# A two-way state-space stage: backward states turned in place, entering products read from the states, block-local kernels laid out twice in memory

## The chip, the cores and the metric

One Trainium2 chip, one of its cores. The metric is the device time of one execution in microseconds; the time before is the median of three runs. The kernel is one launch that holds a whole two-layer encoder trunk.

## The reference, cut to what matters

The trunk is an attention layer and then a two-way diagonal state-space layer over 1024 prompt and 256 sample tokens of width 1024. Only the second layer's core is concerned. For each of 64 groups of 16 channels a scan runs forward and another backward over the tokens:

```
bu_re = einsum('btgc,gpc->btgp', uc, bb_re)      # and bu_im
_, _, hr, hi = associative_scan(_complex_affine_combine, (ar_full, ai_full, bu_re, bu_im), axis=1)
y = einsum('btgp,gcp->btgc', hr, c_re) - einsum('btgp,gcp->btgc', hi, c_im)
...
y = (y_fwd + y_bwd) + d * u
gl = gelu(y);  y = gl * sigmoid(gl @ w_glu + b_glu) * silu(z)
```

## The kernel before, in words

`ssm_stage` (line 1291) takes the tokens in columns of L = 8, so 160 columns: 128 of the prompt, 32 of the sample. One group's 8 x 16 inputs of a column fill 128 partitions. What a column adds to its own 8 outputs is a product with a 128 x 128 "near" kernel; what comes from other columns passes through 64 complex states of each direction.

**First half.** TensorE projects the tokens in 16 tiles of weights (eight of u, then eight of z), each in three chunks of tokens and three products of split float32 numbers. ScalarE casts each tile's weights (`w_split`, line 1477); the low parts are subtracted by GpSimd for tiles 0 to 9 and by VectorE for tiles 10 to 15. Each u block of eight groups is stored, read back with 8 x 16 inputs on the partitions, and multiplied into the states that leave each column (`leaving`, line 1612); ScalarE copies the forward half into partitions 0 to 63 of `states`, VectorE the backward half, columns reversed, into partitions 64 to 127. From tile 9 on TensorE also makes the near kernels (`kernels`, line 1627): 16 turns q of four groups, one after each chunk. ScalarE copies a turn out, GpSimd adds the skip term, and SyncE (SP) stores it in `kernel_scratch` and then loads what turn q + 2 needs.

**The scan.** VectorE walks 127 columns (lines 1570 to 1598), both directions at once, prompt and sample together for the first 31. A step is four dependent operations on a column, which lies as 2 x 64 floats, 512 bytes, so a state's next column is 512 bytes further. The walk pauses at steps 0, 12, 31, 43, 59 and 75 for the low weights of tiles 10 to 15; at each pause VectorE waits for ScalarE's cast.

**Second half.** Work goes in 24 joints, three to a block of eight groups (3, 3 and 2 groups). A joint is a near product per group (line 1674: moving u, stationary near kernel, whose weights lie 16 bytes apart) and two entering products per group (line 1691: stationary `e`, moving the entering states). Each joint has a PSUM bank, so the near products of the first eight joints run ahead of the scan's end. For the entering products ScalarE gathers the forward states of a joint from `states` into `en` (`entering`, line 1512) and VectorE the backward states, turned round (lines 1599 to 1608), two joints ahead. Then come gelu and the stores.

SP's order (lines 1421 to 1463) sets when the loads of the second half start: three groups of near kernels, each of eight DMAs to 16 partitions (line 1409), u again block by block (line 1404), the `e` blocks (line 1416), and the stores of y.

Of the kernel before, what the change touches and what calls it, by code (L numbers as in the profile page):

```python
# [54 lines left out]
L = 8  # L55
# [1220 lines left out]
TURN = 4  # L1276
QG = 4
# [13 lines left out]
def ssm_stage(nc, w_d, h_scratch, skip_d, f_scratch, e_scratch, bb_scratch, c0_scratch, decay_scratch,  # L1291
              u_scratch, z_scratch, kernel_scratch, y_scratch):
# [10 lines left out]
    with ExitStack() as ctx:  # L1303
# [8 lines left out]
        with ExitStack() as first:  # L1312
# [26 lines left out]
        en = out_u[:].rearrange("p a t -> p (a t)")[:, 0:2 * PART * 2 * NC]\  # L1339
            .rearrange("p (b g r n) -> p b g r n", b=2, g=PART, r=2)  # L1340
# [9 lines left out]
        k_done, k_out, k_skip, k_stored = (m.sem(n) for n in ("k_done", "k_out", "k_skip", "k_stored"))  # L1350
# [4 lines left out]
        local, enter_f, enter_b, y_done, y_out = (m.sem(n) for n in ("local", "enter_f", "enter_b", "y_done", "y_out"))  # L1355
# [3 lines left out]
        def lo_wait(eng, n):  # L1359

            if n < SCAN_TILE:
                eng.wait_ge(w_lo, n + 1)
            else:
                eng.wait_ge(w_lo_scan, n - SCAN_TILE + 1)

# [6 lines left out]
        def _(sp):  # L1372
# [32 lines left out]

            def near_load(x):
                lo, hi = NEAR_LOADS[x]
                for s in range(L):
                    sp.dma_start(near[s * SC:(s + 1) * SC, 2 * lo:2 * hi],
                                 kernel_scratch[:, 2 * lo:2 * hi, (L - 1 - s) * SC:(2 * L - 1 - s) * SC])\  # L1410
                      .then_inc(near_in[x], 16)
# [11 lines left out]
            for n in range(NT):  # L1423
                if n + 2 < NT:
                    w_load(n + 2)
                for c in range(len(CHUNKS)):
                    if c == len(CHUNKS) - 1:
                        sp.wait_ge(out, 3 * (n + 1))
                        if n < NB:
                            store_u(n)  # L1430
                        else:
                            sp.dma_start(z_scratch[n - KT], ot).then_inc(stored, 16)
                    q = kernels_after(n, c)
                    if q is not None:
                        sp.wait_ge(k_skip, q + 1)
                        sp.dma_start(kernel_scratch[:, q], kk).then_inc(k_stored, 16)
                        if q + 2 < HALVES:
                            kernel_load(q + 2)
                if n == NB:
                    sp.wait_ge(left, SG)  # L1440
                    kernel_load(0)
                    kernel_load(1)
            sp.wait_ge(k_stored, 16 * HALVES)
            sp.wait_ge(done, 3 * NT)
            sp.wait_ge(stored, U_STORED)
            near_load(0)
# [27 lines left out]
        def _(act):  # L1474
# [5 lines left out]

            w_split(0)
# [3 lines left out]
            for n in range(NT):  # L1485
                if n + 1 < NT:
                    w_split(n + 1)
                for c, (lo, cnt) in enumerate(CHUNKS):
# [23 lines left out]
            def entering(j):  # L1512
                if j >= 2:
                    act.wait_ge(y_done, j - 1)
                g = joint_groups(j)
                act.copy(en[0:64, j % 2, 0:len(g)], states[0:64, g[0]:g[-1] + 1]).then_inc(enter_f, 1)

            act.wait_ge(stored, U_STORED)
            act.wait_ge(k_stored, 16 * HALVES)
            act.wait_ge(step, 4 * STEPS_ALL + 1)  # L1520
            entering(0)
            entering(1)
            for j in range(JOINTS):
# [7 lines left out]
                if j + 2 < JOINTS:  # L1531
                    entering(j + 2)
# [19 lines left out]
        def _(dve):  # L1552
# [45 lines left out]
            dve.wait_ge(step, 4 * STEPS_ALL + 1)  # L1598
            dve.wait_ge(stored, U_STORED)
            dve.wait_ge(k_stored, 16 * HALVES)  # L1600
            for j in range(JOINTS):
                if j >= 2:
                    dve.wait_ge(y_done, j - 1)
                g = joint_groups(j)
                src = states[64:128, g[0]:g[-1] + 1]
                dst = en[64:128, j % 2, 0:len(g)]
                dve.tensor_copy(dst[:, :, :, 0:PC], src[:, :, :, 0:PC][:, :, :, ::-1]).then_inc(enter_b, 1)
                dve.tensor_copy(dst[:, :, :, PC:NC], src[:, :, :, PC:NC][:, :, :, ::-1]).then_inc(enter_b, 1)

        @block.tensor  # L1610
        def _(pe):
# [53 lines left out]
            def near_part(j):  # L1665

                b = j // PARTS
                if j % PARTS == 0:
                    pe.wait_ge(u2_in[b % 2], 16 * (b // 2 + 1))
                    for x, (lo, hi) in enumerate(NEAR_LOADS):  # L1670
                        if b == lo:
                            pe.wait_ge(near_in[x], 16 * L)
# [9 lines left out]
            for j in range(JOINTS):  # L1682
# [144 lines left out]
def build(nc, a, y_out):  # L1827
# [3 lines left out]
    with ExitStack() as ctx:  # L1831
# [13 lines left out]
        kernel_scratch = dram("kernel_scratch", [SC, SG // QG, TAPS * SC, QG])  # L1845
        u_scratch = dram("u_scratch", [NB, L, SC, GB, NC])
# [3 lines left out]
        with ExitStack() as held:  # L1850
# [6 lines left out]
                  decay_scratch, u_scratch, z_scratch, kernel_scratch, ys_scratch)  # L1857
# [65 lines left out]
```

## Time and profile before

| | us |
|---|---|
| median of 3 runs (2572.59 to 2580.78) | 2574.89 |
| the profiled execution | 2571.37 |
| its span | 2569.5 |
| TensorE busy over the span | 2337.5 |
| VectorE busy | 1130.2 |
| ScalarE busy | 922.2 |

Times in the rows are microseconds from the span's start. The state-space stage's second half lies from about 2160 to 2277. A float32 product shows in the profile as two pairs of weight load (PEld) and matmul (PE), so every product of the second half counts as two records.

### The profile page before, as it was taken

The numbers are of one execution on the slowest core, as the hardware profiler recorded it, in microseconds if no ns is written. First come the engines' busy times: TensorE is split into PE (matmuls) and PEld (weight loads), VectorE is DVE, ScalarE is ACT, GpSimd is POOL, SyncE is SP. The second block draws the span as 40 slices with busy tenths as digits, with TensorE's granted clock in tenths as the row PEclk, the third lists the DMA queues.
The fourth block names the chain that finished last, engine by engine and source line by source line (L and its number), as shares of the span: only waits on it lengthen the run. The fifth ranks groups of instructions, "written<-read, shape, count | busy, mean of one in ns | idle before, by whom it ended". The sixth has DMA issues, their size and how long they took to land. (4 is left out here: it accounts for less than half of the span.)

```text
span 2569.5 us, 38223 instructions
## 1 busy us (share of the span) xinstructions
PE 2337.5 (91%) x13896; PEld 1877.4 (73%) x13896; DVE 1130.2 (44%) x2686; ACT 922.2 (36%) x2176; POOL 792.9 (31%) x1244
## 2 busy tenths in 40 slices
PE   4999999999999999999999999759699996758788
PEld 3777777777777777777777777448588775657677
DVE  5243353353264254254254245243422688445433
ACT  4233433333433443443343433332344321453222
POOL 0715565465465465466411011010011000001200
PEclk6999999999999999999999999779899998879989
DMA  4221322222222222232122121045455454844433
GB/s 144 64 53 38 86 59 75 68 77 75 68 77 67 67 68 85 58 77 85 52 60 64 37 56 48 2 156 183 183 148 168 148 155 120 246 123 146 144 137 123
DMA packets 185044, 249.69 MB, mean 97 GB/s; under 512 B 85536, under 2 KB 131488, under 8 KB 182688
## 3 DMA queue, kind: packets, MB, share of 16 engines
q1 hardware_dynamic: 184864, 247.30, 32.7%
q8 instruction: 112, 1.84, 0.3%
q14 instruction: 68, 0.56, 0.1%
HBM read 153.23 MB, written 62.55 MB: 84 GB/s over the span
## 5 line engine op out<-in xcount | busy, mean ns | idle before, releaser
L1065 PE MATMUL att_pj<-hT_hi,att_wh 128*128 128x512 f32 (+1 forms) x1920 | 710.0, 370 | 9.9 <-DVE att_wl L847 9.9
L1065 PE MATMUL att_pj<-hT_hi,att_wl 128*128 128x512 f32 (+1 forms) x1920 | 683.6, 356 | 0.0
L1065 PE MATMUL att_pj<-hT_lo,att_wh 128*128 128x512 f32 (+1 forms) x1920 | 682.5, 355 | 0.0
L703 POOL TENSOR_TENSOR att_sw<-att_sw,att_rope 128x1280 f32<-128x1280 f32 x48 | 202.7, 4223 | 762.0 <-DMA att_sw<-att_t 761.9
L1065 PEld LDWEIGHTS att_pj<-hT_hi,att_wh 128*128 128x128 f32 x1920 | 364.2, 190 | 57.5 <-DVE att_wl L847 10.5
L1065 PEld LDWEIGHTS att_pj<-hT_hi,att_wl 128*128 128x128 f32 x1920 | 363.5, 189 | 53.0
L859 DVE CUSTOM_DVE_ANT_0 att_sm<-att_sc,att_mask 128x128 f32<-128x128 f32 (+2 forms) x480 | 152.6, 356 | 560.0 <-PE att_sc L981 558.9
L1065 PEld LDWEIGHTS att_pj<-hT_lo,att_wh 128*128 128x128 f32 x1920 | 364.9, 190 | 45.4
L729 ACT ACTIVATE att_pr<-att_sm,att_stats 128x128 f32<-128x128 f32 (+2 forms) x480 | 214.9, 449 | 440.0 <-PE att_tr L991 312.0
L771 ACT COPY att_t<-att_pj 128x512 f32<-128x512 f32 (+1 forms) x216 | 111.3, 515 | 371.7 <-PE att_pj L1065 371.6
L681 POOL TENSOR_TENSOR att_prod<-att_power,att_ab 128x128 f32<-128x128 f32 x416 | 158.4, 412 | 8.4
L878 DVE TENSOR_TENSOR att_t<-att_t,att_rope 128x1280 f32<-128x1280 f32 x48 | 71.6, 1492 | 202.7 <-DMA att_sw<-att_t 202.7
L869 DVE COPY att_pt<-att_tr 128x512 f32<-128x512 f32 (+1 forms) x192 | 107.1, 558 | 110.0 <-PE att_tr L991 109.8
L153 PE MATMUL ssm_y_ps<-ssm_hh,ssm_wh 128*128 128x512 f32 (+1 forms) x384 | 139.9, 364 | 16.0 <-DVE ssm_hl L1556 16.0
L1004 PE MATMUL att_po<-att_pt,att_val 128*64 128x128 f32 (+1 forms) x1536 | 146.5, 295 | 6.4 <-ACT att_o L750 5.9
L981 PE MATMUL att_sc<-att_qk 64*128 64x128 f32 (+2 forms) x960 | 146.1, 382 | 0.0
L991 PE MATMUL att_tr<-att_ident,att_pr 128*128 128x128 f32 (+1 forms) x768 | 138.8, 294 | 0.0
L154 PE MATMUL ssm_y_ps<-ssm_hl,ssm_wh 128*128 128x512 f32 (+1 forms) x384 | 137.0, 357 | 0.0
L155 PE MATMUL ssm_y_ps<-ssm_hh,ssm_wl 128*128 128x512 f32 (+1 forms) x384 | 136.6, 356 | 0.0
L1004 PEld LDWEIGHTS att_po<-att_pt,att_val 128*64 128x64 f32 (+1 forms) x1536 | 79.0, 136 | 72.8 <-issue 52.9
L890 DVE TENSOR_TENSOR att_qk<-att_t,att_sw 128x1024 f32<-128x1024 f32 (+1 forms) x80 | 107.6, 1381 | 46.8 <-issue 34.6
L981 PEld LDWEIGHTS att_sc<-att_qk 64*128 64x128 f32 x960 | 74.1, 189 | 61.0 <-issue 46.2
(222 smaller groups left out, 3733.1 us busy)
## 6 DMA issues: line engine op xcount, KB each, us to landing
att_raw<-in_w_att_dram SPq DMA_DIRECT2D x80, 512.0 KB, 3.8
att_sw<-att_t SPq DMA_DIRECT2D x192, 160.0 KB, 2.9
f_scratch<-att_ft SPq DMA_DIRECT2D x32, 256.0 KB, 2.4
e_scratch<-att_place SPq DMA_DIRECT2D x8, 1024.0 KB, 4.6
ssm_raw<-in_w_ssm_dram SPq DMA_DIRECT2D x16, 512.0 KB, 6.4
ssm_f<-f_scratch SPq DMA_DIRECT2D x16, 512.0 KB, 5.0
ssm_f<-e_scratch SPq DMA_DIRECT2D x16, 512.0 KB, 3.7
ssm_e<-e_scratch SPq DMA_DIRECT2D x8, 1024.0 KB, 20.0
```

The costliest lines, as they stand in the source:

```text
L153: pe.matmul(out, lh, rh, start=first, stop=False)
L154: pe.matmul(out, lh, rl, start=False, stop=False)
L155: return pe.matmul(out, ll, rh, start=False, stop=last)
L681: pool.tensor_tensor(prod[:, j], old[:, x], y, ALU.mult).then_inc(pool_step, 1)
L703: pool.tensor_tensor(sw[:], sw[:], rope[:, 1], ALU.mult).then_inc(sin_done, 1)
L729: act.activation(pr[:, h, 0:w], sm[:, h, 0:w], ACT.Exp, bias=st[:, unit % 2, s, h, 0:1], scale=-1.0, accum_out=st[:, unit % 2, s, h, 1:2]) ...
L771: act.copy(dst, src).then_inc(chunk_out, 1)
L859: dve.tensor_tensor_reduce(sm[:, h, 0:w], sc[:, h, 0:w], mask[:, x:x + w], -SCALE, 3e38, ALU.add, ALU.min, st[:, unit % 2, s, h, 0:1]).the ...
L981: pe.matmul(sc[:, h, 0:w], qk[head, unit % 2, Q_TILE, s * P:(s + 1) * P], qk[head, unit % 2, K_TILE, k0:k0 + w], start=True, stop=True).th ...
L991: last = pe.transpose(tr[0:k, h, j], pr[:, h, c0:c0 + k], ident[:])
L1004: last = pe.matmul(po[head, 0:P], val[0:k, b, head], pt[0:k, h, j], start=(j == 0), stop=(j == len(pieces) - 1))
L1065: last = pe.matmul(pj[:, c % 3, 0:n], w[:, k % 2, kt], h[:, kt, lo:lo + n], start=(r == 0), stop=(r == CHUNK_MMS - 1))
```

## The change

- **Turning.** After the scan has passed them, ScalarE swaps the backward states end for end in place: `flip`, 20 times, four columns against the four at the mirrored place, three copies of 64 x 512 floats by way of a buffer `held`, each waiting for the one before. Each flip waits for the scan step that finished its later columns. Four flips stand after tile 12, three after tile 14, three after tile 15, ten after the tiles.
- **Entering products** take `states[:, g, ri]` as the moving operand, both directions at once, 160 elements at steps of 512 bytes. The buffer `en` and its copies on ScalarE and VectorE are gone. TensorE waits once, for the last step and the last flip.
- **Kernels spread in memory.** After each four turns SP waits until their stores have landed and issues eight DMAs from memory to memory, which lay the shifted kernels out as the partitions of `near` want them (`near_scratch`). A near load is then one DMA to 128 partitions.

```
+SPREAD = 4
+FLIP = 4
-        en = out_u[:].rearrange("p a t -> p (a t)")[:, 0:2 * PART * 2 * NC]...
+        held = ub[64:128, 0:FLIP * 2 * SG].rearrange("p (n r g) -> p n r g", r=2, g=SG)
...
+        FLIPS = [(PC + x, NC - FLIP - x) for x in range(SCH // 2 - FLIP, -1, -FLIP)] +\
+                [(x, PC - FLIP - x) for x in range(PC // 2 - FLIP, -1, -FLIP)]
+        FLIP_TILE, FLIP_AT = 12, (0, 4, 4, 7, 10)
+        def flip_step(x):
+            last = FLIPS[x][1] + FLIP - 1
+            return min(last + 1, STEPS_ALL) if last < PC else min(last - PC + 1, STEPS_BOTH)
...
+            def spread(x):
+                sp.wait_ge(k_stored, 16 * SPREAD * (x + 1))
+                for s in range(L):
+                    sp.dma_start(near_scratch[s, :, SPREAD * x:SPREAD * (x + 1)],
+                                 kernel_scratch[:, SPREAD * x:SPREAD * (x + 1), (L - 1 - s) * SC:(2 * L - 1 - s) * SC])\
+                      .then_inc(k_spread, 16)
             def near_load(x):
                 lo, hi = NEAR_LOADS[x]
-                for s in range(L):
-                    sp.dma_start(near[s * SC:(s + 1) * SC, 2 * lo:2 * hi],
-                                 kernel_scratch[:, 2 * lo:2 * hi, (L - 1 - s) * SC:(2 * L - 1 - s) * SC])\
-                      .then_inc(near_in[x], 16)
+                sp.dma_start(near[:, 2 * lo:2 * hi],
+                             near_scratch[:, :, 2 * lo:2 * hi].rearrange("s c q n g -> (s c) q n g"))\
+                  .then_inc(near_in[x], 16)
...
                         sp.dma_start(kernel_scratch[:, q], kk).then_inc(k_stored, 16)
+                        if q % SPREAD == SPREAD - 1:
+                            spread(q // SPREAD)
                         if q + 2 < HALVES:
                             kernel_load(q + 2)
...
+            def flip(x):
+                lo, hi = (slice(c, c + FLIP) for c in FLIPS[x])
+                lo_back, hi_back = (slice(c + FLIP - 1, c - 1 if c else None, -1) for c in FLIPS[x])
+                back = st[64:128]
+                act.wait_ge(step, 4 * flip_step(x) + 1)
+                if x >= 1:
+                    act.wait_ge(flipped, 3 * x)
+                act.copy(held, back[:, lo_back]).then_inc(flipped, 1)
+                act.wait_ge(flipped, 3 * x + 1)
+                act.copy(back[:, lo], back[:, hi_back]).then_inc(flipped, 1)
+                act.wait_ge(flipped, 3 * x + 2)
+                act.copy(back[:, hi], held).then_inc(flipped, 1)
...
+                if n >= FLIP_TILE:
+                    for x in range(FLIP_AT[n - FLIP_TILE], FLIP_AT[n - FLIP_TILE + 1]):
+                        flip(x)
+            for x in range(FLIP_AT[-1], len(FLIPS)):
+                flip(x)
...
-                pe.wait_ge(enter_f, j + 1)
-                pe.wait_ge(enter_b, 2 * (j + 1))
+                if j == 0:
+                    pe.wait_ge(step, 4 * STEPS_ALL + 1)
+                    pe.wait_ge(flipped, 3 * len(FLIPS))
...
                         last = pe.matmul(py[:, j % BANKS, x * NC:(x + 1) * NC], e[:, b % E_BUFS, ri, g % GB],
-                                         en[:, j % 2, x, ri], start=False,
+                                         states[:, g, ri], start=False,
                                          stop=(ri == 1 and g == groups[-1]))
```

On ScalarE, between the end of tile 12 and the first chunk of tile 13, the order before is this (the CAST makes the high weights of tile 14, the 16-partition copies take a near kernel out of PSUM):

```order
L1507 COPY ssm_out_u<-ssm_y_ps 16x512
L1509 COPY ssm_out_u<-ssm_y_ps 16x448
L1479 CAST ssm_wh<-ssm_raw 128x1024
L1501 ACTIVATE ssm_out_u<-ssm_y_ps 128x512
L1507 COPY ssm_out_u<-ssm_y_ps 16x512
```

In the changed kernel four flips of three copies stand between the kernel's copy and the CAST; the last two of them are shown (`held` lies in `ssm_out_u`):

```order
L1511 COPY ssm_out_u<-ssm_states 64x512
L1513 COPY ssm_states<-ssm_states 64x512
L1515 COPY ssm_states<-ssm_out_u 64x512
L1511 COPY ssm_out_u<-ssm_states 64x512
L1513 COPY ssm_states<-ssm_states 64x512
L1515 COPY ssm_states<-ssm_out_u 64x512
L1501 CAST ssm_wh<-ssm_raw 128x1024
L1537 ACTIVATE ssm_out_u<-ssm_y_ps 128x512
L1543 COPY ssm_out_u<-ssm_y_ps 16x512
```

The CAST has moved behind twelve copies. On SP, at the store of near kernel q = 3 and the four loads for q = 5, before:

```order
L1436 DMA kernel_scratch<-ssm_out_u 16x960
L1384 DMA ssm_f<-e_scratch 128x2x512
L1385 DMA ssm_more<-bb_scratch 128x2x64
L1386 DMA ssm_more<-c_scratch 128x2x64
L1387 DMA ssm_more<-in_skip_dram 16x64
```

and in the changed kernel:

```order
L1455 DMA kernel_scratch<-ssm_out_u 16x960
L1422 DMA near_scratch<-kernel_scratch 16x4x512 x8
L1396 DMA ssm_f<-e_scratch 128x2x512
L1397 DMA ssm_more<-bb_scratch 128x2x64
L1398 DMA ssm_more<-c_scratch 128x2x64
L1399 DMA ssm_more<-in_skip_dram 16x64
```

The four loads have moved behind a wait for the store and eight DMAs; the same stands at q = 7, 11 and 15.

## Rows read from the trace of the kernel before

**Rows 1.** Windows: length; PE, PEld, DVE, ACT, POOL busy (instructions); PEclk; DMA share; GB/s.

```profile
2163.00:2180.00 17.00, 0.52 (x2) 0.55 (x3) 15.23 (x60) 0.00 (x0) 0.00 (x0) 0.55 0.98 172
2180.00:2194.00 14.00, 7.86 (x32) 7.64 (x30) 12.86 (x45) 1.98 (x2) 0.00 (x0) 0.74 1.04 320
2194.00:2225.00 31.00, 18.07 (x98) 17.64 (x99) 10.90 (x14) 14.91 (x14) 0.00 (x0) 0.83 1.05 279
2225.00:2259.00 34.00, 33.83 (x192) 33.59 (x191) 17.30 (x23) 22.43 (x22) 0.00 (x0) 0.94 0.54 150
```

**Rows 2.** Timeline of PE, second half: start, length, line, records, [idle before, releaser].

```profile
2179.48 8.38 PE L1674 MATMUL ssm_y_ps<-ssm_u,ssm_near 128*128 128x160 f32 x32 [19.60 <-DMA ssm_u<-u_scratch]
2194.36 3.59 PE L1674 MATMUL ssm_y_ps<-ssm_u,ssm_near 128*128 128x160 f32 x12 [6.50 <-DMA ssm_u<-u_scratch]
2197.74 3.89 PE L1691 MATMUL ssm_y_ps<-ssm_out_u,ssm_e 128*128 128x160 f32 x24
...
2224.57 1.96 PE L1674 MATMUL ssm_y_ps<-ssm_u,ssm_near 128*128 128x160 f32 x6 [10.58 <-DMA ssm_u<-u_scratch]
...
2237.48 1.56 PE L1674 MATMUL ssm_y_ps<-ssm_u,ssm_near 128*128 128x160 f32 x6
2238.88 1.79 PE L1691 MATMUL ssm_y_ps<-ssm_out_u,ssm_e 128*128 128x160 f32 x12
2240.51 1.09 PE L1674 MATMUL ssm_y_ps<-ssm_u,ssm_near 128*128 128x160 f32 x4
...
2267.61 3.04 PE L1691 MATMUL ssm_y_ps<-ssm_out_u,ssm_e 128*128 128x160 f32 x20 [0.15 <-ACT ssm_out_u L1516]
```

**Rows 3.** Timeline of SP's queue at kernel q = 3.

```profile
2048.23 0.31 SPq L1436 DMA_DIRECT2D kernel_scratch<-ssm_out_u  x1
...
2050.51 0.60 SPq L1387 DMA_DIRECT2D ssm_more<-in_skip_dram  x1
```

**Rows 4.** DMA issues from 2044 to 2062: KB each, median us to landing.

```profile
kernel_scratch<-ssm_out_u SPq DMA_DIRECT2D x2, 60.0 KB, 1.8
...
ssm_more<-in_skip_dram SPq DMA_DIRECT2D x1, 4.0 KB, 3.0
```

**Rows 5.** Timeline of weight loads: the first of kernel q = 5.

```profile
2058.16 0.16 PEld L1637 LDWEIGHTS ssm_y_ps<-ssm_more 128*16 128x16 f32 x4
```

**Rows 6.** Timeline of SP's queue, second half.

```profile
2163.34 3.63 SPq L1409 DMA_DIRECT2D ssm_near<-kernel_scratch  x8
...
2202.60 1.67 SPq L1404 DMA_DIRECT2D ssm_u<-u_scratch  x1
```

**Rows 7.** Groups of ScalarE by form: count, busy us, mean ns, idle before.

```profile
L1516 ACT COPY ssm_out_u<-ssm_states 64x960 f32<-64x960 f32 x16 | 29.2, 1834 | 31.7 <-DVE ssm_states L1582 31.7
L1516 ACT COPY ssm_out_u<-ssm_states 64x640 f32<-64x640 f32 x8 | 10.3, 1292 | 0.0
...
L1501 ACT ACTIVATE ssm_out_u<-ssm_y_ps 128x512 f32<-128x512 f32 x16 | 9.6, 597 | 63.9 <-PE ssm_y_ps L155 63.9
```

**Rows 8.** Timeline of ScalarE: the cast of tile 14.

```profile
2107.37 1.04 ACT L1479 CAST ssm_wh<-ssm_raw 128x1024 fp32r<-128x1024 f32 x1
```

**Rows 9.** Timeline of VectorE: scan steps 59 and 127, pauses at 59 and 75.

```profile
2106.28 0.29 DVE L1582 TENSOR_TENSOR ssm_states<-ssm_states,ssm_t 128x128 f32 x1
2108.45 1.23 DVE L1596 TENSOR_TENSOR ssm_wl<-ssm_raw,ssm_wh 128x1024 fp32r<-128x1024 f32 x1 [1.87 <-ACT ssm_wh L1479]
...
2131.15 1.22 DVE L1596 TENSOR_TENSOR ssm_wl<-ssm_raw,ssm_wh 128x1024 fp32r<-128x1024 f32 x1 [2.93 <-ACT ssm_wh L1479]
...
2191.62 0.29 DVE L1582 TENSOR_TENSOR ssm_states<-ssm_states,ssm_t 128x128 f32 x1
```

**Rows 10.** Groups of weight loads from 2175 to 2275: busy us, mean ns.

```profile
L1691 PEld LDWEIGHTS ssm_y_ps<-ssm_out_u,ssm_e 128*128 128x128 f32 x256 | 38.3, 200 | 3.0 <-issue 2.1 <-ACT ssm_out_u L1516 0.8
L1674 PEld LDWEIGHTS ssm_y_ps<-ssm_u,ssm_near 128*128 128x128 f32 x128 | 32.3, 328 | 39.5 <-issue 32.8 <-DMA ssm_u<-u_scratch 6.7
```

More of the change, by code:

```diff
@@ L1291, in ssm_stage @@
 def ssm_stage(nc, w_d, h_scratch, skip_d, f_scratch, e_scratch, bb_scratch, c0_scratch, decay_scratch,
-              u_scratch, z_scratch, kernel_scratch, y_scratch):
+              u_scratch, z_scratch, kernel_scratch, near_scratch, y_scratch):
     NT = 2 * KT
@@ L1337, in ssm_stage @@
         skip_by_tap = [v.rearrange("p g c -> p c g") for v in sk]
-        en = out_u[:].rearrange("p a t -> p (a t)")[:, 0:2 * PART * 2 * NC]\
-            .rearrange("p (b g r n) -> p b g r n", b=2, g=PART, r=2)
+        held = ub[64:128, 0:FLIP * 2 * SG].rearrange("p (n r g) -> p n r g", r=2, g=SG)
         py = m.ps("y_ps", [P, BANKS, 512])
@@ L1349, in ssm_stage @@
         k_in = [m.sem(f"k_in{b}") for b in range(2)]
-        k_done, k_out, k_skip, k_stored = (m.sem(n) for n in ("k_done", "k_out", "k_skip", "k_stored"))
+        k_done, k_out, k_skip, k_stored, k_spread = (m.sem(n) for n in ("k_done", "k_out", "k_skip", "k_stored",
+                                                                        "k_spread"))
         w_lo_scan = m.sem("w_lo_scan")
@@ L1354, in ssm_stage @@
         u2_in, y_stored = ([m.sem(f"{n}{b}") for b in range(2)] for n in ("u2_in", "y_stored"))
-        local, enter_f, enter_b, y_done, y_out = (m.sem(n) for n in ("local", "enter_f", "enter_b", "y_done", "y_out"))
+        local, flipped, y_done, y_out = (m.sem(n) for n in ("local", "flipped", "y_done", "y_out"))
         NEAR_LOADS = ((0, 3), (3, 6), (6, NB))
@@ L1445, in _ @@
             sp.wait_ge(stored, U_STORED)
+            sp.wait_ge(k_spread, 16 * L * (HALVES // SPREAD))
             near_load(0)
@@ L1510, in _ @@
                                  [:, 0:(L - 1) * SC]).then_inc(k_out, 1)
[L1512 to L1522, printed above, removed]
+                if n >= FLIP_TILE:
[3 more added lines that the diff above has]
+                flip(x)
             for j in range(JOINTS):
@@ L1530, in _ @@
                                ACT.Gelu_apprx_tanh).then_inc(y_out, 1)
-                if j + 2 < JOINTS:
-                    entering(j + 2)
         @block.gpsimd
@@ L1597, in _ @@
                 steps(first, end, 2 if first < STEPS_BOTH else 1)
[L1598 to L1608, printed above, removed]
         @block.tensor
@@ L1671, in near_part @@
                         if b == lo:
-                            pe.wait_ge(near_in[x], 16 * L)
+                            pe.wait_ge(near_in[x], 16)
                 for x, g in enumerate(joint_groups(j)):
@@ L1845, in build @@
         kernel_scratch = dram("kernel_scratch", [SC, SG // QG, TAPS * SC, QG])
+        near_scratch = dram("near_scratch", [L, SC, SG // QG, P, QG])
         u_scratch = dram("u_scratch", [NB, L, SC, GB, NC])
@@ L1856, in build @@
         ssm_stage(nc, a["w_ssm"], h2_scratch, a["skip"], f_scratch, e_scratch, bb_scratch, c0_scratch,
-                  decay_scratch, u_scratch, z_scratch, kernel_scratch, ys_scratch)
+                  decay_scratch, u_scratch, z_scratch, kernel_scratch, near_scratch, ys_scratch)
         with ExitStack() as held:
```

## The prediction, made blind

> **What bounds the kernel now.** I read the state-space stage's tail first, stretch by stretch, because only there does the change touch the path that sets the end; then TensorE's own timeline of that tail, then the queue and the two engines that release it. By stretches [rows 1]: TensorE is busy 0.52 of 17 us from 2163, 7.86 of 14 from 2180, 18.07 of 31 from 2194, and then 33.83 of 34 us from 2225. So up to 2225 TensorE waits, and after that it is itself the bound. TensorE's timeline [rows 2] says for what. A float32 matmul shows as two records, so the near products of a joint of three groups are 6 records and its entering products 12. The near products of the first eight joints (32 + 12 records) wait 19.60 us and 6.50 us for u; the entering products start at 2197.74; the block-4 near products wait 10.58 us for u before 2224.57; the last entering product ends at 2267.61 + 3.04 = 2270.65. Everything behind that point (the last gelu, eight stores, the gated stage) is untouched, so what I forecast is the shift of that 2270.65.
>
> Unhindered [rows 2], 6 near records take 2238.88 - 2237.48 = 1.40 us, 0.233 each, and 12 entering records 2240.51 - 2238.88 = 1.63 us, 0.136 each. Per block of eight groups that is 16 x 0.233 + 32 x 0.136 = 8.1 us: TensorE's floor, with the gathering copies on ScalarE and VectorE beside it.
>
> **The change, part by part.** The sum is against the profiled execution's 2571.37 us, which is 3.5 below the median shown, 2574.89.
>
> 1. *Spreading the kernels, 32 DMAs of 128 KB.* Each of the four spreads stands on SP between a kernel store and the load for the kernel two turns on. Before, the store of q = 3 goes at 2048.23, the last of the four loads for q = 5 at 2050.51 [rows 3]; that lands 3.0 us later [rows 4], 2053.5, and TensorE takes it up at 2058.16 [rows 5]: 4.6 us of slack. Now SP first waits for the store to land (1.8 us [rows 4]), then issues eight DMAs; eight of the like took 3.63 us [rows 6]. That is 5.4 us later, so 0.8 us of stall from issue alone; besides, 1 MB of pieces of 2 KB lies ahead in the queues, which at the 172 GB/s of the near loads [rows 1] is 6 us of transfer, partly under the issue. I take 3 us of stall, bounds 1 and 5. The same holds for q = 7; the third spread has a longer chunk behind it and the fourth is followed by no load, both nothing. So TensorE's projections run 2 to 10 us late, I take **6**. At the projections' own end this is covered: the near loads that follow them go at 2163.34 [rows 6], 28 us before the scan ends. What it delays is below.
>
> 2. *Turning the states, 60 copies of 64 x 512 on ScalarE.* The nearest row is a ScalarE pass over 512 elements without steps, 597 ns [rows 7]; with its wait for the copy before I take 0.65 us (0.6 to 0.8), 1.95 per flip. Four flips stand between tile 12 and the cast of the weights of tile 14, all with their steps long done, so they run at once: 4 x 1.95 = 7.8 us (7.2 to 9.6). Queued behind them is the cast, and VectorE waits for the cast in the middle of the scan: before, scan step 59 ends at 2106.57 and VectorE idles 1.87 us until the cast of 2107.37 is done [rows 8, 9]. So the scan moves by the whole 6 + **7.8** us. At its next pause, where it idled 2.93 us for the cast of tile 15 [rows 9], it now comes late and does not wait: **-2.9**. The scan's last step, ending at 2191.62 + 0.29 = 2191.9 [rows 9], ends at 2202.8. The other 16 flips come after tiles 14 and 15 and after the projections; they follow the scan, four steps (4.7 us) for every flip of 1.95 us, and delay nothing. Only the last stands behind the last step: entering products may start at 2202.8 + **1.95** = 2204.8, 7.0 us later than now.
>
> 3. *Near kernels in three DMAs over 128 partitions instead of 24 over 16.* SP's eight issues of 3.63 us become one, and 1.5 MB that moved at 172 GB/s should move as the weights of the entering products did (320 GB/s in the stretch where those prevail [rows 1]). The first eight joints' near products then need neither wait of [rows 2]. Worth nothing here: they are done before 2204.8, and u for block 4, which landed at 2224.57 because its load was issued at 2202.60 [rows 6] behind 4 MB, is needed now only after five joints. If the entering products are quick, this is where their gain comes from (first rival).
>
> 4. *Entering products from the states, one element every 512 bytes.* 256 records. No row shows TensorE streaming a moving operand in steps, so I bound it. Below: 0.136, as now; below that is excluded, columns and weights being the same. Nearest above, on the same engine: the near kernels are stationary operands with a step of 16 bytes, the entering weights have none, both 128 columns: 328 against 200 ns per load [rows 10], and near records are spaced by 0.233 us, 0.233 / 128 = 1.82 ns per column. ScalarE, reading these very states at 512 bytes, pays (1834 - 1292) / 320 = 1.69 ns per element [rows 7] where its 512 elements without steps took at most 597 / 512 = 1.17. Two engines pay much the same per stepped element, which speaks for a limit in the memory. At 1.75 ns a record of 160 columns takes 0.28 us; if both passes of a float32 record read anew, 0.56. I take **0.28**: 256 x 0.28 = 71.7 us instead of 34.8. Near products left after the first eight joints: 84 x 0.233 = 19.6 us, as now.
>
>    The Trainium skill's page "SBUF — State Buffer" (section "Door 1: The DMA port swizzle", its note on cachelines) says that accesses in one 16-byte line run at full bandwidth and each access to a new line pays; it prices nothing, and by it the products slow down. The rows on the stationary operand and on ScalarE agree; none shows a moving operand.
>
> 5. *Removed:* 24 copies on ScalarE and 48 on VectorE. They were beside TensorE's floor but for the first (between 2191.9 and 2197.74, where u was later still) and some 2 us at the end. Nothing more.
>
> **Sum.** 2204.8 + 71.7 + 19.6 = 2296.1 against 2270.65: **+25.4**, so 2571.4 + 25.4 = **2597**. TensorE is then never short of data in the tail. Own range of this case: stalls 2 to 10, records 0.27 to 0.29: 2590 to 2604.
>
> **Rivals.**
> - *Stepped moving reads are free (faster).* TensorE would have its floor, 54.4 us, with none of the waits for u: 2204.8 + 54.4 = 2259.2, -11.5: 2560; with the smallest stalls 2556, with shorter flips too 2555. For it: a record takes its columns slowly, 0.136 / 160 = 0.85 ns each, and TensorE's moving side may fetch ahead in that time. Against: the stationary operand on the same engine pays. It decides if a record stays under about 0.18 us (256 x 0.045 = 11.5). The Trainium skill's "TensorE: Matmul & The Clock Gate" (section "Step-by-step: what each phase is for") says a stream of N columns takes N cycles whatever is read; by that this rival holds.
> - *Every pass reads anew.* 0.56 per record: 71.7 us more, 2669. For it: nothing but that a record makes two passes over its columns; against: 160 stepped reads already fill 0.28 us.
> - *Partly hidden.* Records near 0.19 us, so loss and gain cancel: 256 x 0.19 = 48.6, 2204.8 + 48.6 + 19.6 = 2273, +2.4: 2574. This is also where the change would not do what it says, the gap filled and the time the same.
>
> **How the numbers follow.** Forecast 0.62; free 0.22; anew 0.10; partly hidden 0.06. About 0.3%, 7.7 us, is what a measurement of this kernel can tell from no change. Free lies wholly below 2567, partly hidden inside, the forecast and anew above: faster 0.22, same 0.06, slower 0.72. The range takes in the free case and the forecast's own and leaves out anew: 2554 to 2608.
>
> **What would show it.** The line of the entering products: records spaced 0.27 to 0.29 us (0.14 free, 0.55 anew). The scan's last step near 2203, with VectorE idle some 14 us more before the fifth weight subtraction of the scan and no idle before the sixth. Two waits of TensorE for the kernel loads, 1 to 5 us each, after q = 3 and q = 7. Near loads landing within 8 us, and no wait of TensorE for u. I am wrong if the entering products are spaced as before; half wrong if the scan ends before 2196, the flips or the spreads then costing nothing.

## The result, and the profile after

The changed kernel takes **2594.77 us** (median of 4 runs, 2593.48 to 2598.86) against 2573.74 us for the kernel before on the same chip (4 runs, 2569.93 to 2580.78): a ratio of **1.008**, 95% interval 1.0064 to 1.0095, slower by about 21 us. The profiled execution took 2593.48 us with a span of 2591.6; it is compared with the one before, 2571.37.

The windows of the change's second half, columns as in [rows 1], with one stretch more at the end:

```profile
2163.00:2180.00 17.00, 5.05 (x34) 4.61 (x33) 15.22 (x60) 12.04 (x20) 0.00 (x0) 0.76 0.55 212
2180.00:2194.00 14.00, 10.83 (x44) 10.61 (x42) 12.56 (x50) 7.38 (x12) 0.00 (x0) 0.74 1.01 421
2194.00:2225.00 31.00, 18.86 (x73) 16.55 (x73) 9.50 (x37) 8.96 (x14) 0.00 (x0) 0.70 0.68 249
2225.00:2259.00 34.00, 34.00 (x137) 28.75 (x137) 0.00 (x0) 4.73 (x9) 0.00 (x0) 1.00 0.47 116
2259.00:2295.00 36.00, 35.47 (x135) 27.85 (x133) 0.00 (x0) 5.75 (x11) 0.00 (x0) 1.00 0.28 55
```

From 2225 on TensorE is busy 34.00 of 34 us and gets the full clock (granted 1.00), yet it does 137 records there where it did 192 before, and it needs nearly another 36 us. VectorE's and ScalarE's gathering is gone, and the DMA engines are no busier than before (a share of 0.47 against 0.54). That points to the pace of TensorE's records. Its own timeline (as [rows 2]):

```profile
2179.41 8.41 PE L1691 MATMUL ssm_y_ps<-ssm_u,ssm_near 128*128 128x160 f32 x32 [11.95 <-DMA ssm_u<-u_scratch]
2190.99 3.46 PE L1691 MATMUL ssm_y_ps<-ssm_u,ssm_near 128*128 128x160 f32 x12 [3.17 <-DMA ssm_u<-u_scratch]
2206.59 6.82 PE L1709 MATMUL ssm_y_ps<-ssm_states,ssm_e 128*128 128x160 f32 x24 [12.14 <-ACT ssm_states L1515]
...
2216.23 1.46 PE L1691 MATMUL ssm_y_ps<-ssm_u,ssm_near 128*128 128x160 f32 x6
2217.53 3.44 PE L1709 MATMUL ssm_y_ps<-ssm_states,ssm_e 128*128 128x160 f32 x12
2220.80 1.46 PE L1691 MATMUL ssm_y_ps<-ssm_u,ssm_near 128*128 128x160 f32 x6
...
2274.66 19.81 PE L1709 MATMUL ssm_y_ps<-ssm_states,ssm_e 128*128 128x160 f32 x72
```

Twelve entering records take 2220.80 - 2217.53 = 3.27 us, **0.2725 us each**, where they took 0.136. Six near records take 1.30 us, 0.217 each. The products start at 2206.59, when ScalarE's last flip ends, and the last one ends at 2274.66 + 19.81 = 2294.47. No wait for u stands between them.

A low clock would look the same, so it has to be ruled out. In the kernel before, twelve entering records without a step took 2229.47 - 2226.32 = 3.15 us, 0.2625 each, right behind the wait of 10.58 us for u; the granted clock was 0.50 from 2226.4 to 2229.4, the level of 1.2 GHz:

```profile
2226.32 3.32 PE L1691 MATMUL ssm_y_ps<-ssm_out_u,ssm_e 128*128 128x160 f32 x12
2229.47 1.50 PE L1674 MATMUL ssm_y_ps<-ssm_u,ssm_near 128*128 128x160 f32 x6
```

In the change the twelve records at 2217.53 ran at 1.00. Its first 24, from 2206.59 to 2213.23, ran at 0.50 up to 2212 and took 0.277 each, hardly more than the 0.2725 at the full clock. So the low clock is not what makes them slow, and a record with the step takes nearly the same time at either level.

What moved the start is seen on four engines. SP's timeline (as [rows 3] and [rows 6]):

```profile
2047.48 0.31 SPq L1455 DMA_DIRECT2D kernel_scratch<-ssm_out_u  x1
2049.34 5.09 SPq L1422 DMA_DIRECT2D near_scratch<-kernel_scratch  x8
...
2056.45 0.60 SPq L1399 DMA_DIRECT2D ssm_more<-in_skip_dram  x1
...
2083.21 5.84 SPq L1422 DMA_DIRECT2D near_scratch<-kernel_scratch  x8
...
2091.06 0.60 SPq L1399 DMA_DIRECT2D ssm_more<-in_skip_dram  x1
2091.70 0.42 SPq L1451 DMA_DIRECT2D z_scratch<-ssm_out_u  x1
```

The last load for kernel q = 5 now goes 9.0 us after the store of q = 3, where it went 2.3 us after it [rows 3]. TensorE's weight loads of the kernels that wait for it, q = 5 (as [rows 5]) and q = 9:

```profile
2059.95 0.16 PEld L1654 LDWEIGHTS ssm_y_ps<-ssm_more 128*16 128x16 f32 x4 [2.67 <-DMA ssm_more<-in_skip_dram]
...
2094.81 0.18 PEld L1654 LDWEIGHTS ssm_y_ps<-ssm_more 128*16 128x16 f32 x4 [4.06 <-DMA ssm_more<-in_skip_dram]
```

ScalarE (as [rows 8]) makes its four flips and only then the cast of tile 14; before that it waited for a z store that had stood behind the spreads:

```profile
2096.28 0.60 ACT L1537 ACTIVATE ssm_out_u<-ssm_y_ps 128x512 f32<-128x512 f32 x1 [8.76 <-DMA z_scratch<-ssm_out_u]
...
2114.94 0.62 ACT L1511 COPY ssm_out_u<-ssm_states 64x512 f32<-64x512 f32 x1
2115.58 0.62 ACT L1513 COPY ssm_states<-ssm_states 64x512 f32<-64x512 f32 x1
...
2122.87 1.05 ACT L1501 CAST ssm_wh<-ssm_raw 128x1024 fp32r<-128x1024 f32 x1
...
2205.83 0.61 ACT L1515 COPY ssm_states<-ssm_out_u 64x512 f32<-64x512 f32 x1
```

And VectorE (as [rows 9]) waits for that cast, but no longer for the next one. The first line is the second weight subtraction of the scan; in the kernel before it began at 2040.33, with a wait of 6.33 us:

```profile
2039.59 1.23 DVE L1624 TENSOR_TENSOR ssm_wl<-ssm_raw,ssm_wh 128x1024 fp32r<-128x1024 f32 x1 [3.82 <-ACT ssm_wh L1501]
...
2123.95 1.23 DVE L1624 TENSOR_TENSOR ssm_wl<-ssm_raw,ssm_wh 128x1024 fp32r<-128x1024 f32 x1 [16.99 <-ACT ssm_wh L1501]
2143.76 1.22 DVE L1624 TENSOR_TENSOR ssm_wl<-ssm_raw,ssm_wh 128x1024 fp32r<-128x1024 f32 x1
...
2204.21 0.29 DVE L1610 TENSOR_TENSOR ssm_states<-ssm_states,ssm_t 128x128 f32 x1
```

**Where the 22.1 us between the two profiled executions are.** The scan began 1.6 us later in this execution, as its first weight subtraction shows (2015.04 against 2013.42). From there to the end of the last step it took 189.5 us instead of 178.5: +11.0. From that end to the first entering product it is 2.1 us instead of 5.8: -3.7. The entering phase, from the first entering product to the end of the last, takes 87.9 us instead of 72.9: +15.0. The rest of the span takes 297.1 us instead of 298.9: -1.8.

Since the start of the scan differs by a few us from one execution to the next, the runs below are read by lengths of their own profile: **scan** (first weight subtraction of the scan to the end of its last step) and **entering phase**. The scan's first stretch differs too, from 24.6 us (after) to 27.4 (e9_rows), by how long VectorE waits for the second cast. The first spread and the first flip come later than that, so it is no doing of the change. The column **from the second** therefore counts from the second weight subtraction (2204.5 - 2039.59 = 164.9 for the change).

| run | scan, us | from the second, us | entering phase, us | median, us |
|---|---|---|---|---|
| before | 178.5 | 151.6 | 72.9 | 2573.74 |
| after | 189.5 | 164.9 | 87.9 | 2594.77 |
| e1_contig | 194.3 | 167.1 | 55.9 | 2568.86 |
| e2_spread | 187.8 | 162.5 | 59.5 | 2568.04 |
| e3_turn | 183.9 | 156.7 | 91.5 | 2589.52 |
| e4_cast | 187.0 | 159.9 | 87.9 | 2596.77 |
| e5_load | 184.0 | 156.7 | 87.9 | 2586.50 |
| e6_gather | 178.8 | 151.6 | 59.7 | 2556.38 |
| e8_pairs | 177.8 | 151.6 | 59.4 | 2552.74 |
| e9_rows | 178.9 | 151.6 | 53.5 | 2547.28 |

The kernel before took 2572.45, 2572.57 and 2570.26 us (medians) beside e1 to e4, e5 to e8 and e9. One execution of it beside e5 to e8 took 4569.17 us, was in the slow state, and counts in no ratio.

### The profile page after: what moved, and what is told of

It is laid out like the page before. It is cut to its first block and busy times, and to the rows that moved or that the text cites. A ratio compares the mean times of both kernels' runs of the same rounds, so it can differ in the third digit from the quotient of the medians.

```text
span 2591.6 us, 38217 instructions
## 1 busy us (share of the span) xinstructions
PE 2367.4 (91%) x13896; PEld 1893.8 (73%) x13896; DVE 1096.3 (42%) x2638; ACT 922.6 (36%) x2212; POOL 794.9 (31%) x1244
```

## The experiments

### The step alone: e1_contig

```
-                                         states[:, g, ri], start=False,
+                                         st[:].rearrange("p n r g -> p (n r g)")[:, (2 * g + ri) * NC:(2 * g + ri + 1) * NC], start=False,
```

> The changed kernel with one thing altered: each entering product reads 160 neighbouring floats of the same states tile (a different piece for each group and part) instead of 160 floats 512 bytes apart, so the entering terms of the output are computed from other data. Theory (each stepped element costs the moving side of TensorE about 1.7 ns): records fall from 0.272 to 0.136 us, the last entering product ends near 2261 instead of 2294, the time is about 2561, unless the wait for u returns. Rival (the products are slow because of what else changed in them, such as both directions lying in a tile that two engines write, and not because of the step): records stay at 0.27, about 2595.

Measured: 2568.86 us (10 runs, 2564.2 to 2574.44), ratio 0.9989 (0.9979 to 0.9999). TensorE's timeline of this run:

```profile
2208.63 4.87 PE L1709 MATMUL ssm_y_ps<-ssm_states,ssm_e 128*128 128x160 f32 x24 [9.19 <-ACT ssm_states L1515]
...
2224.82 1.79 PE L1709 MATMUL ssm_y_ps<-ssm_states,ssm_e 128*128 128x160 f32 x12
2226.45 1.56 PE L1691 MATMUL ssm_y_ps<-ssm_u,ssm_near 128*128 128x160 f32 x6
...
2254.61 9.94 PE L1709 MATMUL ssm_y_ps<-ssm_states,ssm_e 128*128 128x160 f32 x72
```

Twelve records take 1.63 us again, 0.136 each, with every instruction, wait and buffer of the change in place: the step is the whole of the 32 us by which the entering phase differs. The time came out 8 us above the theory's: in this profile the scan ended 2.1 us later than in the change's, the entering phase took 1.5 us more than the 54.4 without waits, the untouched rest of the span 3.1 us more, and the median lies 2.2 us above the profiled execution. Flips and spreads together cost 15.5 us of scan here, 13.3 in the profile of the change (from the second subtraction on). So even where stepped reads were free, the change as written would have gained only 0.1%.

### The spreads alone: e2_spread

The kernel before with `near_scratch`, the spreads and the near load of one DMA; gathering, `en` and the copies as before.

```
+                        if q % SPREAD == SPREAD - 1:
+                            spread(q // SPREAD)
...
-                for s in range(L):
-                    sp.dma_start(near[s * SC:(s + 1) * SC, 2 * lo:2 * hi],
+                sp.dma_start(near[:, 2 * lo:2 * hi],
+                             near_scratch[:, :, 2 * lo:2 * hi].rearrange("s c q n g -> (s c) q n g"))\
```

> The kernel before with only the spread kernels and the three near loads of one DMA each; gathering copies and entering products as before. Theory (the late u of the tail came from near loads that moved slowly to 16 partitions; the spreads stall TensorE some 6 us during the projections, of which 3 reach the scan's end): scan ends near 2195, first entering product near 2197, no wait for u above 1 us, last entering product near 2252 instead of 2270.7, about 2556. Rival (the 7 MB of e blocks hold the queues, the near loads do not matter): the wait of 10 us for u stays, 2570 to 2577.

Measured: 2568.04 us (9 runs, 2563.33 to 2570.08), ratio 0.998 (0.9971 to 0.999). Both halves of the account are there. The entering phase falls from 72.9 to 59.5 us, since no entering or near product waits for u any more. The scan grows from 178.5 to 187.8 us (by 10.9 from the second subtraction on), so most of that is given back. Weight loads of this run:

```profile
2064.97 0.16 PEld L1649 LDWEIGHTS ssm_y_ps<-ssm_more 128*16 128x16 f32 x4 [3.23 <-DMA ssm_more<-in_skip_dram]
...
2101.24 0.18 PEld L1649 LDWEIGHTS ssm_y_ps<-ssm_more 128*16 128x16 f32 x4 [4.23 <-DMA ssm_more<-in_skip_dram]
```

These are the same two kernels, q = 5 and q = 9. The theory's scan end of 2195 was wrong: the spreads cost more than I had put on them.

### The flips and stepped reads without the spreads: e3_turn

The change without `near_scratch`, `spread` and its waits; the near loads are the 24 of before.

```
-                        if q % SPREAD == SPREAD - 1:
-                            spread(q // SPREAD)
...
-                sp.dma_start(near[:, 2 * lo:2 * hi],
-                             near_scratch[:, :, 2 * lo:2 * hi].rearrange("s c q n g -> (s c) q n g"))\
+                for s in range(L):
+                    sp.dma_start(near[s * SC:(s + 1) * SC, 2 * lo:2 * hi],
```

> The changed kernel without the spreads: near kernels loaded by 24 DMAs as before, turning and stepped entering products kept. Theory: scan ends 5 us later than before (four flips of 1.95 us ahead of the cast, less 2.9 us of a wait that goes), entering products at 0.272 us a record, a wait for u of some 8 us returns because the near loads are slow again; last entering product near 2295, about 2598. Rival (the spreads are dear and their near loads worth nothing): 2589, no wait for u.

Measured: 2589.52 us (4 runs, 2588.47 to 2595.8), ratio 1.0075 (1.0058 to 1.0093). The scan takes 183.9 us, 5.4 more than before (5.1 from the second subtraction on), which is the flips' own price. VectorE's first late pause in this run, and the one wait of TensorE for u:

```profile
2115.85 1.22 DVE L1612 TENSOR_TENSOR ssm_wl<-ssm_raw,ssm_wh 128x1024 fp32r<-128x1024 f32 x1 [9.92 <-ACT ssm_wh L1489]
```

```profile
2223.39 1.96 PE L1679 MATMUL ssm_y_ps<-ssm_u,ssm_near 128*128 128x160 f32 x6 [3.00 <-DMA ssm_u<-u_scratch]
```

The wait for u is 3.0 us, not 8: slow entering products leave the old loads most of the time they need. So a wait did come back, as the theory had it, but the time is the rival's. The entering phase is 3.6 us longer than with the spreads, and the spreads cost 8.2 us of scan (164.9 - 156.7), so by the profiles they are a loss as placed, beside stepped reads. The times point the same way, but their intervals overlap.

### The flips behind the cast: e4_cast

```
+                if n > FLIP_TILE:
+                    for x in range(FLIP_AT[n - 1 - FLIP_TILE], FLIP_AT[n - FLIP_TILE]):
+                        flip(x)
                 for c, (lo, cnt) in enumerate(CHUNKS):
```

(and the same calls taken out behind the chunks).

> The changed kernel with the flips of a tile moved behind the next tile's cast (four between the cast of tile 14 and the first chunk of tile 13, three after the start of tile 15, thirteen after the tiles). Theory (four flips hold the cast and the cast holds the scan): VectorE's wait before the fifth subtraction falls from 17.0 to about 9 us, a wait of about 3 us returns before the sixth, the scan ends about 5 us sooner, about 2590. Rival (the scan's late end is the spreads' doing alone): 2595, the scan's end unmoved.

Measured: 2596.77 us (6 runs, 2586.73 to 2599.28), ratio 1.0091 (1.0073 to 1.0108). In its profile VectorE waits 6.21 us at this pause and 4.35 at the next, where the change had 16.99 and none. From the second subtraction on the scan takes 159.9 us instead of 164.9, so the 5 us that were expected are there; what is left above the kernel before, 8.3 us, is about what the spreads cost in the change (8.2). The mechanism is the one named, but the time shows nothing of it: the runs lie 12.6 us apart, more than the effect. Inconclusive as a time.

### Loads ahead of the spreads: e5_load and e6_gather

One edit, in the change (e5_load) and in e2_spread (e6_gather):

```
-                        if q % SPREAD == SPREAD - 1:
-                            spread(q // SPREAD)
                         if q + 2 < HALVES:
                             kernel_load(q + 2)
+                        if q % SPREAD == SPREAD - 1:
+                            spread(q // SPREAD)
```

> The change with one edit: at every fourth kernel the next kernel load goes to SP's queue ahead of the eight spreads, not behind them. Theory (the projection is stretched because the loads of B, C, E and D stand behind 5 us of spread issue): TensorE's waits for in_skip in the kernels' matmuls, 7.2 + 6.1 + 1.3 us in the change, fall below 3 us in all; from the first pause's subtraction to the scan's last step it takes 184 to 186 us instead of 189.5; the z store of the spread's tile is still pushed back; time 2588 to 2591. Rival (what stretches the projection is the z store behind the spreads, or the spreads' own traffic): those waits may go, but the 189.5 us stay and the time is 2594 to 2596.

> The kernel before with the spreads and the near load of one DMA (as the run e2_spread, 2568.0 us), and the next kernel load ahead of the eight spreads. Theory (late loads): no wait for in_skip of over 1 us in the kernels' matmuls (7.5 + 2.1 before), from the first pause's subtraction to the scan's last step 182 to 184 us instead of 187.8, the entering products 59 to 60 us as in e2_spread, time 2562 to 2565. Rival (z store or traffic): 187 to 188 us, time 2567 to 2569.

Measured: e5_load 2586.5 us (4 runs, 2586.18 to 2589.45), ratio 1.0057 (1.0035 to 1.0078); e6_gather 2556.38 us (6 runs, 2555.74 to 2558.38), ratio 0.9938 (0.9922 to 0.9953). In neither does TensorE wait for in_skip behind a spread any more (one wait ahead of the first spread stays, 2.85 and 2.78 us; the kernel before has it too, with 2.36). e5's scan takes 184.0 us, the same as e3's without any spreads, though ScalarE still waits 6.8 us for the z store behind them; from the second subtraction on both take 156.7. e6's scan takes 178.8 us, as before the change, though ScalarE waits 6.6 us for the z store; from the second subtraction on both take 151.6. VectorE's pauses in e6 are those of [rows 9] to 0.06 us:

```profile
2111.65 1.23 DVE L1608 TENSOR_TENSOR ssm_wl<-ssm_raw,ssm_wh 128x1024 fp32r<-128x1024 f32 x1 [1.93 <-ACT ssm_wh L1491]
2134.36 1.23 DVE L1608 TENSOR_TENSOR ssm_wl<-ssm_raw,ssm_wh 128x1024 fp32r<-128x1024 f32 x1 [2.93 <-ACT ssm_wh L1491]
...
2194.83 0.29 DVE L1594 TENSOR_TENSOR ssm_states<-ssm_states,ssm_t 128x128 f32 x1
```

So the late loads are the whole price of the spreads. The rival falls: the z store behind the spreads and their traffic cost nothing that the scan shows. e6 went past the theory, since with the loads ahead nothing is left, where I had allowed some 4 us.

The late loads cost more than the waits themselves. Behind its second wait in the change TensorE ran at the low clock, where the kernel before was granted 1.00 throughout (columns as in [rows 1]):

```profile
2094.80:2100.00 5.20, 5.18 (x50) 3.30 (x51) 4.70 (x19) 1.31 (x3) 0.00 (x0) 0.50 0.80 240
```

Up to the cast of tile 14, counted from the second subtraction, the change is 8.2 us behind e5: 6.1 are its two waits (2.47 and 3.64 us on the matmuls), 2.1 the slower records behind them. In e1_contig and e2_spread the clock fell behind both waits. e1 is 10.3 us behind e5 at that cast and e2 10.2 behind e6, of which waits are 6.7 and 6.8. In e5 and e6 the granted clock stays at 1.00 from 2040 to 2160.

### Spreads two by two: e8_pairs

```
                         if q + 2 < HALVES:
                             kernel_load(q + 2)
-                        if q % SPREAD == SPREAD - 1:
-                            spread(q // SPREAD)
+                        if q >= SPREAD:
+                            spread(q // SPREAD - 1, range(q % SPREAD * L // SPREAD, (q % SPREAD + 1) * L // SPREAD))
...
             sp.wait_ge(k_stored, 16 * HALVES)
+            spread(HALVES // SPREAD - 1)
```

> The same, but the eight spreads of a set are not issued in a row: two of them follow each of the next four kernel loads, and only the last set goes out in a row, behind the last kernel. So neither a kernel load nor a z store stands behind more than two spreads (some 1.4 us of issue). Theory (what the spreads cost is the order of SP's queue): from the first pause's subtraction to the scan's last step 179 to 181 us (178.5 in the kernel before), entering products 59 to 60 us, time 2557 to 2561, the fastest of all. Rival (the spreads' traffic itself costs, wherever it is issued): 185 us or more, time 2565 or more.

Measured: 2552.74 us (6 runs, 2549.54 to 2557.09), ratio **0.9919** (0.9902 to 0.9936). The wait for the z store is gone too, the scan takes 177.8 us, the entering phase 59.4. That is less than the theory's time, but the intervals of e6 and e8 overlap, and from the second subtraction on both scans take 151.6 us, so these runs show no gain of pairs over eight in a row behind the load.

### The size of the step: e7_steps

```
+APART = (128, 1, 2, 3, 4, 8, 32, 128)
...
-                                         states[:, g, ri], start=False,
+                                         st[:].rearrange("p n r g -> p (n r g)")[:, 0:(NC - 1) * APART[b] + 1:APART[b]], start=False,
```

> The change, but the entering products of block b read their 160 columns from the first group's row of the states at steps of 512, 4, 8, 12, 16, 32, 128 and 512 bytes for b = 0 to 7 (so y is made of other data; the instructions are the same in number, order and shape). Theory (what costs is how many pieces of 16 bytes a row touches): 0.136 us a record at steps of 4 and 8 bytes, 0.18 to 0.22 at 12, 0.272 at 16 and at every step above. Rival A (any step but 4 bytes costs the same): 0.272 from 8 bytes on. Rival B (the price grows with the distance): still 0.136 at 16 and 32 bytes, and 0.272 first at 128 or 512. At 32 records a block: theory some 4.4 us for each cheap block and 8.7 for each dear one.

Measured: 2588.22 us, one run. TensorE's timeline; between the rows shown lie the other joints of each block, with the same lengths:

```profile
2220.53 1.79 PE L1710 MATMUL ssm_y_ps<-ssm_states,ssm_e 128*128 128x160 f32 x12
2222.16 1.56 PE L1692 MATMUL ssm_y_ps<-ssm_u,ssm_near 128*128 128x160 f32 x6
...
2228.61 1.85 PE L1710 MATMUL ssm_y_ps<-ssm_states,ssm_e 128*128 128x160 f32 x12
2230.29 1.55 PE L1692 MATMUL ssm_y_ps<-ssm_u,ssm_near 128*128 128x160 f32 x6
...
2236.83 2.73 PE L1710 MATMUL ssm_y_ps<-ssm_states,ssm_e 128*128 128x160 f32 x12
2239.38 1.48 PE L1692 MATMUL ssm_y_ps<-ssm_u,ssm_near 128*128 128x160 f32 x6
...
2247.12 3.57 PE L1710 MATMUL ssm_y_ps<-ssm_states,ssm_e 128*128 128x160 f32 x12
2250.51 1.46 PE L1692 MATMUL ssm_y_ps<-ssm_u,ssm_near 128*128 128x160 f32 x6
...
2259.59 3.63 PE L1710 MATMUL ssm_y_ps<-ssm_states,ssm_e 128*128 128x160 f32 x12
2263.05 1.46 PE L1692 MATMUL ssm_y_ps<-ssm_u,ssm_near 128*128 128x160 f32 x6
...
2268.63 19.96 PE L1710 MATMUL ssm_y_ps<-ssm_states,ssm_e 128*128 128x160 f32 x72
```

From each pair of rows, the twelve records of blocks 1 to 5:

| step, bytes | 4 | 8 | 12 | 16 | 32 |
|---|---|---|---|---|---|
| us per record | 0.136 | 0.140 | 0.2125 | 0.2825 | 0.288 |
| pieces of 16 bytes touched | 40 | 80 | 120 | 160 | 160 |

The last row, 72 records at 32, 128 and 512 bytes, gives 19.96 / 72 = 0.277. Rival A falls on 8 bytes, rival B on 16. At 12 bytes it is 0.2125 / 120 = 1.77 ns per piece, at 16 bytes 0.2825 / 160 = 1.77, at 512 bytes 0.2725 / 160 = 1.70. At 8 bytes 80 pieces at 1.75 ns are 0.14 us, just what the 160 columns take anyway. These spacings, all at a granted clock of 1.00, fit one rule: a record takes the longer of 0.85 ns per column and some 1.75 ns per piece of 16 bytes.

### Near weights without a step: e9_rows

The run e8_pairs with the kernels kept group by group, in the scratch memory and in `near`.

```
-        near = m.sb("near", [P, HALVES, P, QG])
+        near = m.sb("near", [P, HALVES, QG, P])
...
-        kk = ub[0:SC, 0:QG * TAPS * SC].rearrange("p (n g) -> p n g", g=QG)
+        kk = ub[0:SC, 0:QG * TAPS * SC].rearrange("p (g n) -> p g n", g=QG)
...
-                    last = pe.matmul(py[:, j % BANKS, x * NC:(x + 1) * NC], near[:, g // QG, :, g % QG], u2[:, b % 2, g % GB],
+                    last = pe.matmul(py[:, j % BANKS, x * NC:(x + 1) * NC], near[:, g // QG, g % QG], u2[:, b % 2, g % GB],
```

> The run e8_pairs (2552.7 us, entering phase 59.4 us from 2197.93 to 2257.32) with the kernels kept group by group: TensorE reads its near weights without a step instead of every 16 bytes, and the spreads and the near loads move pieces of 512 bytes instead of 2 KB. Theory (the price per piece of 16 bytes holds for TensorE's weights too, and it is what spaces near records by 0.233 us): near records at 0.136 to 0.15, entering phase 51 to 55 us (84 near records by 0.09 is 7.6 us, part of it lost to waits for the gathering copies), time 2545 to 2550. Rival A (near records are spaced by something else): 0.22 to 0.24 as before, 2552 to 2554. Rival B (the smaller pieces make the near loads so late that they set the start): entering products start some us after 2198 with a wait for a load, time 2555 or more.

Measured: 2547.28 us (5 runs, 2540.54 to 2548.65), ratio **0.9899** (0.9881 to 0.9916). TensorE's timeline:

```profile
2194.27 5.17 PE L1704 MATMUL ssm_y_ps<-ssm_out_u,ssm_e 128*128 128x160 f32 x24 [2.20 <-ACT ssm_out_u L1529]
...
2203.60 0.98 PE L1687 MATMUL ssm_y_ps<-ssm_u,ssm_near 128*128 128x160 f32 x6
2204.42 1.79 PE L1704 MATMUL ssm_y_ps<-ssm_out_u,ssm_e 128*128 128x160 f32 x12
...
2244.72 3.04 PE L1704 MATMUL ssm_y_ps<-ssm_out_u,ssm_e 128*128 128x160 f32 x20 [0.15 <-ACT ssm_out_u L1529]
```

Six near records take 0.82 us, 0.137 each instead of 0.233, and the entering phase ends after 53.5 us instead of 59.4. Both rivals fall. The spacing of 0.233 us between near records was the price of weights that lie 16 bytes apart. This is the lowest median of the study, 1% below the kernel before; its interval overlaps that of e8_pairs, and what sets it apart is the entering phase, 5.9 us shorter. It keeps the change's spreads, behind the loads, and leaves out its flips and stepped reads.

## Why the prediction was right

The forecast held: 2597 us was said, 2594.77 measured, on the side and by the mechanism named. By its own steps:

1. **Spreads.** Said: two stalls of TensorE after q = 3 and q = 7, 3 us each, 6 in all. The places were right and the waits too: the weight loads waited 2.67 and 4.06 us, the matmuls 2.47 and 3.64. The price was not: from the second subtraction on the change's scan takes 8.2 us more than e5_load's (164.9 - 156.7), because the low clock behind the second wait came on top, for which the sum had no term. The parts were off as well: eight DMAs from memory to memory took SP 5.1 to 5.8 us to issue, not the 3.63 of the near loads [rows 6], while the two in_skip loads were taken up 3.5 and 3.8 us after their issue, against a landing in 3.0 [rows 4], so little is seen of the queueing that I had added. The price also varies between executions: 8.2 us here, 10.4 in e1_contig, whose program is the same up to the entering products, 10.9 in e2 against e6. That the whole scan grew by 11.0 us, where 10.9 was the forecast, was luck: its stretch up to the second subtraction, which nothing of the change reaches, happened to be 2.4 us shorter than in the profile of before. I had not reckoned with ScalarE's 8.76 us for the z store; by e6 it costs nothing.
2. **Flips.** Said: 0.65 us a copy, four flips 7.8 us ahead of the cast, 2.9 regained at the next pause, so 4.9 net. Copies start 0.65 us apart, the four flips take 2122.87 - 2114.94 = 7.9 us, the next pause has no wait, and e3_turn, without spreads, gives 5.1 us net (from the second subtraction on). The scan was to end at 2202.8 and ended at 2204.5.
3. **Near loads.** Said: the first near products need neither wait. They still waited 11.95 and 3.17 us for u, since the loads could go only at 2171.33, 8.0 us later than before [rows 6], and the first two of near took 8.2 us to land, the third 14.5; so that sign failed, though it was worth nothing, as said. That u for block 4 would be no bound came out.
4. **Stepped reads.** Said: 0.28 us a record, by 1.75 ns per element from rows of TensorE's own weights and of ScalarE. Measured 0.2725, so 256 records cost 69.8 us and not 71.7; near records took 0.217 instead of 0.233, another 1.4 us less. These two make the 3.4 us by which the entering phase (87.9) is shorter than the 91.3 of the sum, and the difference of the totals (22.1, profile to profile, against 25.4), since the later start of the entering products (2206.59 against 2204.8: +1.8) and the shorter rest (-1.8) cancel.

   The note on cachelines in the Trainium skill's page "SBUF — State Buffer" (section "Door 1: The DMA port swizzle") has each access to a new 16-byte line pay unless a line is hit at least twice; e7_steps agrees, two hits at 8 bytes being free and 12 bytes not, and adds the price of about 1.75 ns. The note's "4 fp32" as the stride that is free is more than was measured: a step of three float32 took 0.2125 us a record, of four 0.2825.
5. **Rivals.** *Free* fell in the profile of the change itself; e1_contig shows the kernel that it described, at 2568.9 us and not 2560, of which 3.8 us are the later start of its entering products (2208.63 against 2204.8). The rule of the Trainium skill's "TensorE: Matmul & The Clock Gate" (section "Step-by-step: what each phase is for"), N columns in N cycles, gives a step no price; e7_steps agrees with that up to steps of 8 bytes and not above, and the 0.85 ns that a column takes there is two cycles of 2.4 GHz, not one. *Read anew* would have shown 0.55 us a record, *partly hidden* 0.19; neither did.

What the large edit lost is so named: 32.0 us by the steps (87.9 against the 55.9 of e1_contig) and 13.3 us of scan, 8.2 by the spreads and 5.1 by the flips; against it stand 17.0 us in the entering phase, mostly waits for u (72.9 - 55.9), and 3.7 us ahead of it. The spreads alone remove 13.2 and 3.8 of these (e6). (256 records by 0.2725 - 0.136 are 35 us. The 32.0 are less, as the first 24 run at the low clock, where the step costs little, and the near records come a little closer together.)

## What to carry to other kernels

The step of a float32 moving operand is paid by 16-byte pieces: steps up to 8 bytes are free, from 16 bytes on the records here took twice as long at the full clock, so a gathering copy on an engine that has time is the better deal. Weights pay too, though only a step of 16 bytes was measured (0.233 us a record against 0.137 without), and they were better laid out without a step even though that made smaller DMA pieces (e9). When transfers are added to a queue, put what an engine waits for ahead of them: one swap of two statements was worth 8 to 12 us here (e5, e6). Judge the parts of a change apart, since one of the three, once issued behind the loads, is a gain of 0.6 to 0.8% (e6, e8) that the other two hid. And compare executions between two marks behind which the change acts: the first stretch of the scan, which it doesn't reach, varied by 2.8 us and made the spreads look cheaper than they are.

## What was not expected of the hardware

- A moving operand at steps of 8 bytes takes 0.140 us a record against 0.136 without a step, and 12 bytes 0.2125: the price goes by lines touched, not by whether there is a step. Steps of 16 and 32 bytes (0.2825 and 0.288) are a little dearer than 512 (0.2725).
- The time of a record with a step hardly follows TensorE's clock: at 512 bytes it was 0.277 us at a granted 0.50 (the 24 records of the change from 2206.59, the last 1.2 us at 0.73) and 0.2725 at 1.00, while without a step it was 0.2625 and 0.136. At the low clock the step costs next to nothing.
- After waits of 2.5 to 4.2 us for a late load the granted clock of TensorE fell to 0.50 in some cases (behind the 3.64 us in the change) and not in others (behind its 2.47 us); where it fell, the records behind the wait were slower for some us.
- Issuing eight DMAs from memory to memory took SP 5.1 to 5.8 us, 0.64 to 0.73 each. The three sets of eight near loads to 16 partitions in the kernel before took 3.63, 3.73 and 5.01 us, so only the first was clearly quicker.
- The stretch from 2180 to 2194, with the near loads in one DMA over 128 partitions among its transfers, moved 421 GB/s, where the kernel before had 320, and 172 from 2163 to 2180, where its near loads to 16 partitions go out first [rows 1].
